# Hybrid decoder layer on eight cores: the way of three small weight tensors, the place of three value tiles, the order of the last outputs

## The reference, cut to what matters

```python
a = rmsnorm(h, g_mix); z = a @ w_in                   # q | k | v | r | alow | u | vg
log_a = log_sigmoid(alow @ w_a2 + b_a) / 16           # decay, per key channel
S_t = diag(exp(log_a_t)) S_{t-1} + k_t^T v_t ; o_t = q_t S_t
o = rmsnorm(o, g_gla_norm) * silu(r)
vn = layernorm(gelu(vg), g_gmlp_ln, b_gmlp_ln)
m = rmsnorm(gelu(u) * (tril(w_s) @ vn + b_s), g_gmlp_out)   # 8 groups, 128 positions
h = h + concat(o, m) @ w_out
h = h + (silu(gate) * up) @ w_ffn_out
h = h + rmsnorm(p @ w_ple, g_ple) * sigmoid(rmsnorm(h, g_ple_gate) @ w_ple_gate)
y = rmsnorm(h, g_final)
```

## Time and profile before

| | |
|---|---|
| median of 3 runs | 1895.38 us (1892.85 to 1896.1) |
| the profiled execution | 1896.28 us, span of its slowest core 1895.0 us |
| spans of the eight cores | 1884.4 to 1895.0 us |
| busy PE / DVE / ACT / POOL | 1787.0 / 791.1 / 512.5 / 145.1 us |
| mean granted TensorE clock, slowest core | 0.978 |

### The profile page before, as it was taken

The page is one execution under the profiler, slowest core; times in us unless marked ns, Lnnn a source line. Parts: engine busy times, 40 slices in busy tenths (PEclk is TensorE's granted clock), DMA queues, the critical chain, the costliest instruction groups (busy, mean ns, idle before and its releaser), DMA issues.

```text
span 1895.0 us, 26975 instructions; the slowest of 8 cores (1884.4 to 1895.0 us)
## 1 busy us (share of the span) xinstructions
PE 1787.0 (94%) x10027; PEld 951.3 (50%) x10124; DVE 791.1 (42%) x1239; ACT 512.5 (27%) x924; POOL 145.1 (8%) x135
## 2 busy tenths in 40 slices
PE   4899889949999999999999999999999999999995
PEld 2464345524454456656565656565656565644442
DVE  6464522732652451151515151515151515186875
ACT  5844323733560240000000100000000000026665
POOL 2001211311200000000000000000000000000000
PEclk9899899979999999999999999999999999999998
DMA  9850485260845544324343333334242424291211
GB/s 260 187 145 23 139 193 122 42 112 1 180 117 138 89 85 77 62 51 84 57 78 62 73 66 68 73 62 80 55 85 50 90 48 89 45 178 47 72 65 74
DMA packets 42199, 171.57 MB, mean 91 GB/s; under 512 B 3156, under 2 KB 4564, under 8 KB 38232
## 3 DMA queue, kind: packets, MB, share of 16 engines
q0 software_dynamic: 29392, 108.94, 32.6%
q1 hardware_dynamic: 12680, 60.90, 9.3%
HBM read 259.90 MB, written 18.87 MB: 147 GB/s over the span
## 4 chain that ended last, share of the span: by engine, by line
PE 86%; DMA 5%; DVE 5%; ACT 2%; issue 2%; DVEq 0%; ACTq 0%; POOLq 0%; POOL 0%; SPq 0%
PE pf L498 84%; DMA arena<-xm 2%; DVE arena L470 2%; DMA arena<-w_sTs 2%; PE pb L508 1%; ACT arena L460 1%; DVE arena L478 1%; DMA sso<-arena 1%; DVE arena L745 1%; DVE pf L478 1%; DMA arena<-st 1%; DMA arena<-w_al 0%; ACT L491 0%; ACT arena L464 0%; DVE arena L467 0%
## 5 line engine op out<-in xcount | busy, mean ns | idle before, releaser
L498 PE MATMUL pf<-arena 128*128 128x512 bf16 (+4 forms) x9255 | 1743.1, 351 | 60.2 <-DVE arena L478 28.3
L498 PEld LDWEIGHTS pf<-arena 128*128 128x128 bf16 (+1 forms) x9352 | 902.6, 99 | 881.4 <-issue 90.2
L470 DVE TENSOR_TENSOR arena<-pf,arena 128x512 f32<-128x512 f32 (+3 forms) x677 | 445.1, 662 | 812.6 <-PE pf L498 745.9
L460 ACT ACTIVATE arena<-pf 128x384 bf16<-128x384 f32 (+4 forms) x310 | 160.5, 525 | 998.2 <-PE pf L498 987.8
L460 ACT ACTIVATE arena<-arena 128x512 f32<-128x512 f32 (+8 forms) x122 | 127.1, 1050 | 133.1 <-DVE arena L470 77.2
L478 DVE SCALAR_TENSOR_TENSOR arena<-arena 128x2048 bf16<-128x2048 f32 (+3 forms) x67 | 118.5, 1775 | 8.6 <-DMA arena<-g_gout 3.0
L190 POOL DMA_DIRECT2D arena<-w_f x55 | 39.1, 712 | 999.8 <-PE pf L498 971.0
L470 DVE TENSOR_TENSOR arena<-arena 128x512 f32<-128x512 f32 (+7 forms) x102 | 79.4, 786 | 77.7 <-ACT arena L460 43.3
L474 POOL TENSOR_TENSOR arena<-arena 128x1024 f32<-128x1024 f32 x31 | 73.6, 2381 | 257.9 <-ACT arena L464 137.1
L464 ACT COPY arena<-pb 128x1024 bf16<-128x1024 bf16 (+1 forms) x62 | 61.8, 1001 | 94.3 <-PE pb L508 94.0
L508 PE MATMUL pb<-arena 128*128 128x128 bf16 x772 | 59.2, 229 | 26.3 <-DVE arena L478 16.9
(11 more groups left out here) (34 smaller groups left out, 127.9 us busy)
## 6 DMA issues: line engine op xcount, KB each, us to landing
arena<-w_f POOLq DMA_DIRECT2D x44, 1024.0 KB, 9.5
arena<-w_f POOLq DMA_DIRECT2D x11, 2048.0 KB, 14.8
arena<-xm SPq DMA_DIRECT2D x18, 1024.0 KB, 8.9
arena<-w_tok POOLq DMA_DIRECT2D x8, 2048.0 KB, 24.6
y<-arena SPq DMA_DIRECT2D x18, 512.0 KB, 2.7
arena<-xp SPq DMA_DIRECT2D x8, 1024.0 KB, 18.7
arena<-st SPq DMA_DIRECT2D x16, 512.0 KB, 4.9
sso<-arena SPq DMA_DIRECT2D x16, 512.0 KB, 3.5
```

Of the source, the lines that this page charges most:

```text
L460: S.op("act", lambda: nc.scalar.activation(out=out, in_=in_, func=func, **kw), reads=reads, writes=writes, cost=c_act(n, ptr) + (0.17 if " ...
L470: S.op("dve", lambda: nc.vector.tensor_tensor(out=out, in0=a, in1=b, op=op), reads=reads, writes=writes, cost=c_dve(n, rate))
L498: ins = nc.tensor.matmul(o, lhsT=l, rhs=r, start=st, stop=sp_)
```

## The change

The weights `w_al`, `w_sTs` and `w_sT` are loaded by SP in fp32. `walow` lies in region `RO`, its four copies into `walow4` run on POOL, and the four copies of the gain `gmix` on ACT. Both copies after the transposes of `prev_norm` are on DVE. `own_gen` has three value tiles between the decay and the keys of tiles 4 to 7. The multiplications for `WT` and `Wblk` are a function called after `stage_a(1)`, which also waits for the Gelus of tile 1; `mn` is made after it over `wsb`, and the Square of `stage_a` writes into `vn`. In the last stage `final` is split: `final1` (sum and root), and `final2` (multiplications and stores), due after the mixes of the next tile; the last tile goes in quarters with stores on SP and ACT in turn, and ACT is made to have the square root's table (`to_sqrt`) once the last sigmoid is done. The planner's latency of a transfer is 2.6.

```diff
-        self.pend.append(Op("dma", e, (out, in_), list(reads), list(writes), kb, 2.0, prev, nb, boost + self.bst))
+        self.pend.append(Op("dma", e, (out, in_), list(reads), list(writes), kb, 2.6, prev, nb, boost + self.bst))
...
-        walow, r_ = MI.T([128, 16, 16], BF16)
-        S.dma("pool", walow, w_al, writes=[Bwalow])
+        walow, r_ = RO.T([128, 16, 16], F32)
+        RO.release((RO.lo, RO.hi))
+        S.dma("sp", walow, w_al, writes=[Bwalow], boost=8000.0)
         for c in range(4):
-            DCOPY(walow4[:, :, 32 * c:32 * c + 16], walow, [Bwalow], [Bwalow4], 256)
+            S.op("pool", lambda: nc.gpsimd.tensor_copy(out=walow4[:, :, 32 * c:32 * c + 16], in_=walow), reads=[Bwalow], writes=[Bwalow4],
+                 cost=0.8)
...
-            DCOPY(gmix[:, c * 512:(c + 1) * 512], bg_[c][0][:], [bg_[c][1]], [Bgmix[c]], 512)
+            ACOPY(gmix[:, c * 512:(c + 1) * 512], bg_[c][0][:], [bg_[c][1]], [Bgmix[c]], 512)
...
             norm_p2(xnP[:, t, :], [BxnP[t]], lambda hf: apT[:, psl(t), hf * 8:(hf + 1) * 8, :], BapT[t],
-                    ("act", "dve"))
+                    ("dve", "dve"))
...
             main_decay(1)
+            for t in range(VF):                      # VF = 3
+                yield from v_tile(t)
             yield from main_kq(1)
-            for t in range(8):
+            for t in range(VF, 8):
                 yield from v_tile(t)
...
-        ws8, r_ = MI.T([128, 8, 8], BF16, "r")
-        S.dma("pool", ws8, w_sTs, writes=[Bws8])
+        ws8, r_ = MI.T([128, 8, 8], F32, "r")
+        S.dma("sp", ws8, w_sTs, writes=[Bws8])
...
-        wsb, r_ = MI.T([128, 8, 128], BF16, "r")
-        S.dma("pool", wsb, w_sT, writes=[Bwsb])
-        TT(WT, wsb, tri..., ALU.mult, [Bwsb, Btri], [BWT], 1024)
-        for g in range(8):
-            TT(Wblk[:, g, :]..., ws8[:, g, :]..., blk..., ALU.mult, [Bws8, Bblk], [BWblk], 128)
+        wsb, r_ = MI.T([128, 8, 128], F32, "r")
+        S.dma("sp", wsb, w_sT, writes=[Bwsb])
         MI.release(m_ws)
-        mn, Bmn = pair([128, 1024], BF16, "mn")
+        def spatial_weights():
+            TT(WT, wsb, tri..., ALU.mult, [Bwsb, Btri] + Bgv[1], [BWT], 1024)
+            for g in range(8):
+                TT(Wblk[:, g, :]..., ws8[:, g, :]..., blk..., ALU.mult, [Bws8, Bblk] + Bgv[1], [BWblk], 128)
...
-            ACT(mn[t % 2], gv[t], AF.Square, Bgv[t], [Bmn[t % 2], Bst[t][2]], 1024, ...)
+            ACT(vn[t % 2], gv[t], AF.Square, Bgv[t], [Bvn[t % 2], Bst[t][2]], 1024, ...)
...
             stage_a(t)
+            if t == 1:
+                spatial_weights()
             if t % 3 == 2:
                 stage_s(t - 2, t + 1)
+        mn, Bmn = pair([128, 1024], BF16, "mn")
...
-            for half in range(2):
-                ... STT of 1024 columns, store by SP
+        def final2(t):
+            w = 1024 if t < 8 else 512
+            for q in range(D // w):
+                ... STT of w columns, store by "sp" if q % 2 == 0 or t < 8 else "act"
+        def to_sqrt(b):
+            S.op("act", lambda: nc.scalar.activation(out=pst[0][:, 4:5], in_=pst[0][:, 4:5], func=AF.Sqrt, bias=EPS, scale=1.0),
+                 reads=[Bpst[0], b], writes=[Bpst[0]], cost=0.2, tab="sqrt")
...
-            at(b + TP + 8, final, t)
+            if t == NT - 1:
+                at(b + TP - 1, to_sqrt, Bsig[sigs[(t, order_[3])]])
+            at(b + TP + 5.5 if t < 8 else b + TP + 8, final1, t)
+            at(b + TP + 22 if t < 8 else b + TP + 9, final2, t)
```

More of the change, by code:

```diff
@@ L26 @@
 TABLE = 1.3
+VF = 3
 SAMPLE_BOOST = 0.0
@@ L549, in build_nc @@
         m_keep = MI.mark()
-        walow, r_ = MI.T([128, 16, 16], BF16)
-        Bwalow = S.buf("walow", r_)
-        S.dma("pool", walow, w_al, writes=[Bwalow])
         m_id = MI.mark()
@@ L589, in build_nc @@
         dset(walow4, Bwalow4, 0.0, 1.2)
+        walow, r_ = RO.T([128, 16, 16], F32)
+        RO.release((RO.lo, RO.hi))
+        Bwalow = S.buf("walow", r_)
+        S.dma("sp", walow, w_al, writes=[Bwalow], boost=8000.0)
         for c in range(4):
-            DCOPY(walow4[:, :, 32 * c:32 * c + 16], walow, [Bwalow], [Bwalow4], 256)
+            S.op("pool", lambda: nc.gpsimd.tensor_copy(out=walow4[:, :, 32 * c:32 * c + 16], in_=walow), reads=[Bwalow], writes=[Bwalow4],
+                 cost=0.8)
         wa2b, r_ = MI.T([128, 128], F32)
@@ L1158, in build_nc @@
         m_ws = MI.mark()
-        wsb, r_ = MI.T([128, 8, 128], BF16, "r")
+        wsb, r_ = MI.T([128, 8, 128], F32, "r")
         Bwsb = S.buf("wsb", r_)
-        S.dma("pool", wsb, w_sT, writes=[Bwsb])
-        TT(WT, wsb, tri.unsqueeze(1).to_broadcast([128, 8, 128]), ALU.mult, [Bwsb, Btri], [BWT], 1024)
-        for g in range(8):
-            TT(Wblk[:, g, :].rearrange("p (j t) -> p j t", j=16), ws8[:, g, :].unsqueeze(1).to_broadcast([128, 16, 8]),
-               blk.rearrange("p (j t) -> p j t", j=16), ALU.mult, [Bws8, Bblk], [BWblk], 128)
-        MI.release(m_ws)
-        mn, Bmn = pair([128, 1024], BF16, "mn")
+        S.dma("sp", wsb, w_sT, writes=[Bwsb])
+        MI.release(m_ws)
+        def spatial_weights():
+            TT(WT, wsb, tri.unsqueeze(1).to_broadcast([128, 8, 128]), ALU.mult, [Bwsb, Btri] + Bgv[1], [BWT], 1024)
+            for g in range(8):
+                TT(Wblk[:, g, :].rearrange("p (j t) -> p j t", j=16), ws8[:, g, :].unsqueeze(1).to_broadcast([128, 16, 8]),
+                   blk.rearrange("p (j t) -> p j t", j=16), ALU.mult, [Bws8, Bblk] + Bgv[1], [BWblk], 128)
         BcatM = S.bufs(NT, "catM")
@@ L1175, in stage_a @@
                     512, accum_out=st[:, half, t:t + 1])
-            ACT(mn[t % 2], gv[t], AF.Square, Bgv[t], [Bmn[t % 2], Bst[t][2]], 1024, scale=1.0 / 32, accum_out=st[:, 2, t:t + 1])
+            ACT(vn[t % 2], gv[t], AF.Square, Bgv[t], [Bvn[t % 2], Bst[t][2]], 1024, scale=1.0 / 32, accum_out=st[:, 2, t:t + 1])
         def stage_s(t0, t1):
@@ L1475, in mix, with final1 @@
             ACT(sig[i], hs, AF.Square, [Bh[t][db]], [Bsig[i], Bfss[t]], 512, scale=float(D) ** -0.5, accum_out=fss[:, t, db:db + 1])
-        def final(t):
+        def final1(t):
             S.op("dve", lambda: nc.vector.reduce_sum(out=fss[:, t, 4:5], in_=fss[:, t, 0:4], axis=AX.X), reads=[Bfss[t]],
@@ L1480, in final @@
             RSTD(fss[:, t, 5:6], fss[:, t, 4:5], [Bfss[t]], [Bfss[t]])
-            for half in range(2):
[L1482 to L1485, removed]
+        def final2(t):
+            w = 1024 if t < 8 else 512
+            for q in range(D // w):
+                hs = h[t][:, q * w:(q + 1) * w]
+                Bhh = Bh[t][q * w // 512:(q + 1) * w // 512]
+                STT(hs, hs, fss[:, t, 5:6], gfin[:, q * w:(q + 1) * w], ALU.mult, ALU.mult, Bhh + [Bfss[t], Bgfin], Bhh, w)
+                S.dma("sp" if q % 2 == 0 or t < 8 else "act", y[t * 128:(t + 1) * 128, q * w:(q + 1) * w], hs, reads=Bhh, key=Bhh[0])
+        def to_sqrt(b):
+            S.op("act", lambda: nc.scalar.activation(out=pst[0][:, 4:5], in_=pst[0][:, 4:5], func=AF.Sqrt, bias=EPS, scale=1.0),
+                 reads=[Bpst[0], b], writes=[Bpst[0]], cost=0.2, tab="sqrt")
         order_ = (0, 1, 3, 2)
```

## The result

The changed kernel takes 1841.9 us where the one before takes 1895.7 on the same chip: ratio 0.9713, 95% interval 0.9694 to 0.9732, 54 us less. The forecast was 1854.0 with a range of 1845 to 1868. The direction is right, the time lies 3 us under the range, and 12 us more were won than the sum has.

The account below looks back on a forecast made before the run. PE is 86% of the chain, so only its idle or slow-clock time can be won: 29.7 + 5.4 + 2.5 + 3.8 = 41.4 us, from a median of 1895.38 to 1854.0, range 1845 to 1868.

Parts of the forecast that it names:

- Spatial weights: In `stage_a`, PE's hole of 27.2 us and 3.0 of slow clock go, 0.5 is lost at mixing: 29.7 us.
- `spo`'s margin: In `stage_a`, `spo` lands at 414.6 and PE runs to 422.0 before it needs a bank from ACT: 7.4 us.
- (b): In `stage_a`, `spo` takes the place of w_sTs: 5.4 us idle and 1 to 2 of slow clock, 1861; chance 0.06.
- (c): On SP's queue, w_sTs goes behind b_ln, so the first mixing is 10 to 25 us late: 1870 to 1880; chance 0.06.
- (d): w_sTs behind b_ln on SP's queue and its landing takes 30.8 us, until 477: slower, about 1899; chance 0.03.
- The priced loss at the mixing: Before the first mixing, `stage_b(0)` waits for the Square that now writes `vn[0]`: 0.5 us lost, from 0 to 4.
- Three value tiles: In stage 2, the first hole (4.75) and slow matmuls (1.3) go, ACT costs 0.6: 5.4 us, bounds -1 to 11.
- Head: At the kernel's start, first multiplication 1.5 to 2 us and first decay product 4 to 6 sooner: 2.5, from -3 to 6.
- (a): In the early stages the x and state loads rule, head and value tiles give nothing: 7.9 less, 1862; chance 0.14.
- The end: Last stage: 0.9 from DVE's order, 1.3 from `to_sqrt`, quarters, and 1.0 of PE's short waits: 3.8, from 1 to 5.5.
- The quarters: Last tile's stores: 0.1 more on DVE, last store 256 KB and not 512, winning 0.7, between 0 and 1.3.
- Latency 2.6: Planner's transfer latency over the whole kernel: the ties it reorders elsewhere priced at 0, with +-3 us.

Follow-up runs that it names:

- The experiment with the transposes ahead: Changed kernel with the transposes of `o_out(6)` and `o_out(7)` put ahead in the planner's order: 0.9687 of the kernel before, 1837.4 us.
- the run with the head alone: Kernel before with only `w_al` by SP, POOL copies, `gmix` on ACT and both copies after `prev_norm`'s transposes on DVE: 0.9968, 6.1 us faster.
- the run with 2.0: Changed kernel with the planner's latency of a transfer back at 2.0 in place of 2.6: 0.9723 of the kernel before, 52.5 us faster.
- The four parts alone: Kernel before with one part each: value tiles 0.9912, spatial weights 0.9851, last stage 0.9973, first stage's copies and loads 0.9968.

## Why the prediction was wrong by 12 us

**Bound and method.** Right: the chain is PE to 91% now, and all that was won ahead of PE's last product was idle time or slow clock of PE.

**Spatial weights, 29.7 forecast.** 28.4 alone. The hole, the clock, `spo`'s margin (ACT waited 7.72 us for it, PE had none to wait for there) and SP's order are as forecast; rivals (b), (c) and (d) did not come. Rival (b)'s landing was 16.6 us, against the 18.0 of the earlier trace rows. The priced loss at the mixing, 0.5, is 1.7 us (1.27 + 0.43, where the kernel before waited 0.55), and its cause is not the wait on `vn[0]`: it is the load of `g_gout`, which the prediction did not follow. It counted what SP issues ahead of the weights, and not what the shorter stage leaves too little time for. The experiment with the transposes ahead, which lets that load go out 67 us sooner, won about 3 us, but 2.3 of them are the wait at the end of the recurrence. The prediction has no term for that wait either.

**Three value tiles, 5.4 forecast, 16.7 measured: the step that failed.** The prediction priced the first hole (4.75) and ten slow matmuls (1.3), and of the second hole it said "The nearest row says it stays", with 11 as the most. That was the wrong step. The second hole went, since it was ACT's order that turned a late state into a wait of PE, and the edit moved the value copies away from behind it. The trace had this: the releaser of 4.18 us was an ACT copy, and ACT's list around 253 shows the state's cast in front. I had named the landing as the cause and stopped one step early. The slow clock was the second miss: 1.3 us were priced behind one hole, and the kernel before loses 6.9 us to it in three places, 2.6 and 2.7 behind the two holes and 1.4 from 202 to 205, ahead of both, which the prediction did not see. The bound of 11 had the second hole with its slow clock; what it lacked is that third place, half of the slow clock behind the first hole, and some 2.5 us of shorter waits (11.4 us of idle time in all, of which the two holes are 8.9).

**Head, 2.5 forecast of -3 to 6, 6.1 measured.** The first decay product starts at 29.79 ("29 to 31" was the forecast), and the early start carried: in the run with the head alone PE is busy 139.3 us of the first 170, in the kernel before 135.9, and the recurrence starts 4.2 us sooner (medians). The chain does begin with 32.16 us of `xp` landing, as rival (a) had it, but the exponentials of `prev_decay(1)` no longer stand behind the Square that waited for `xm` until 59.17; with the head alone they start at 60.33, before at 62.49. The four POOL copies took 1.99 us together and were over at 6.9, before DVE's first multiplication at 12.81:

```profile
4.92 1.99 POOL L593 CAST arena<-arena 128x256 bf16<-128x256 f32 x4 [2.92 <-DVE arena L567]
```

So the case that the Trainium skill, SBUF — State Buffer (section "SBUF: two separate sides"), warns of, the port pair held through an instruction, did not arise for these copies, and they neither show nor deny the rule.

**The end, 3.8 forecast, 5.1 alone.** The size is near, the parts are not (medians over the cores). From PE's last product to the sum of tile 8: 12.04 us before, 8.71 after, 3.3 won for the 0.9 forecast. The prediction counted DVE's wait of 0.97 and forgot that tile 7's pair, 2.48, itself stood in the path. From the sum to the last multiplication 2.10 before and 1.79 after: 0.3 for the 1.3 of `to_sqrt`. Its load still stands behind the last Square:

```profile
1829.64 0.19 ACT L461 ACTIVATION_READ_ACCUMULATOR arena<-arena 128x1 f32 x1
1829.91 1.28 ACT L1500 ACT_TABLE_LOAD   x1
```

The condition on the last `sig` tile made it wait for that Square, and the planner can't start it sooner; I had read its due time, not what it reads. Leaving it out changed nothing. The quarters: 2.74 on DVE for 2.48, and 5.06 from there to the end for 4.85, so 0.5 lost where 0.6 was to be won; a last store of 256 KB is not quicker to finish than one of 512. PE's short waits: tiles at the end follow each other in 15.98 us and no longer in 16.48, so over four or five tiles 2 us or a little more for the 1.0.

**Latency 2.6, priced at 0.** 7 us alone, nothing in the total on top of the rest. That the 0 came out is luck: it wins 4.2 us ahead of the recurrence, and about as much is lost behind it, 2.3 us of it in a wait that the changed kernel has and the run with 2.0 does not.

**Carried.** The four parts alone make 56.3 where the sum had 41.4: 11.3 more from the value tiles, 3.6 from the head, 1.3 from the end, and 1.3 less from the spatial weights. The whole is 54 (52.5 without the latency), 2 us less than its parts; the wait at the end of the recurrence alone costs 2.3. The time below the range is not the sum of many small errors: with the value tiles at their measured 16.7 and all other terms as forecast the sum gives 52.7 us and 1842.7, within 1 us of the measured time, because the rest nearly cancels.

## What to carry to other kernels

Follow a wait through the in-order list of the engine that releases it: a late transfer costs the critical engine only if what frees its buffers stands behind the waiting instruction, and then reordering removes a hole that looks like a transfer's. Read the granted clock in stretches of 2 us, not as a mean over 20 or 30: PE loses its busy time there times the missing share of the clock, and a low stretch need not have a large hole just ahead of it. When a stage becomes shorter, look at each load that is issued in it and used in the next one, and at what a "due early" instruction really reads. And when the total agrees with the forecast, look for waits that are new: one that an unforeseen gain has paid for is the next thing to win.

## What the runs showed of the hardware

Behind a hole of 4.75 us PE's granted clock was 0.50 until about 222, though PE was busy, and 1.00 from 223 on; in the same stretch without the hole it was 1.00 throughout. A mean of 0.94 over 219 to 250 is this: 4 us at the lower level and 27 at the full one. After the wait of 2.29 us at 369 the clock fell on some cores only: from 355 to 400 it is 0.96 on two of the eight and 1.00 on the others. Transfers of SP beside 4 MB of weight loads took 10 to 17 us whatever their size (sizes in KB, us from issue to landing, in the changed kernel):

```profile
arena<-b_ln SPq DMA_DIRECT2D x1, 512.0 KB, 3.3
arena<-g_gout SPq DMA_DIRECT2D x1, 512.0 KB, 14.8
...
arena<-w_sTs SPq DMA_DIRECT2D x1, 32.0 KB, 10.1
arena<-b_sT SPq DMA_DIRECT2D x1, 8.0 KB, 14.0
```

8 KB took 14.0 us and the 512 KB of `spo` 16.6; the 512 KB of `b_ln`, issued at 428.10 when no weight load was under way, took 3.3.
